# Split weight slots moved from 64 to 48 bytes above the split activations in the address modulo 256, in a two-block transformer kernel

## The chip, the cores and the metric

One core of a Trainium2 chip runs the whole program. The time is the device time of one execution in microseconds. Where a number is called a profiled one it comes from a single execution taken by the hardware profiler.

## What is computed

The reference runs two small models one after the other on one sequence of 256 tokens and 1024 features, all in float32. Nearly all the arithmetic is in products of a 256-row activation with a weight matrix of 1024 or 2816 rows:

```python
def first_block(x, ...):              # layer 0: fox attention, layer 1: NSA attention
    h = rmsnorm(x, norm_g[i])
    y = fox_mixer(...) or nsa_mixer(...)   # h @ w_in, attention, o @ w_out
    x = x + y
...
def _conv_ffn(h, w_up, conv_w, conv_b, w_down):   # after an HGRN mixer and after an MLA mixer
    u = h @ w_up                       # 1024 -> 2 x 2816
    y = causal 3-tap convolution of u
    gate, up = jnp.split(y, 2, axis=-1)
    return (jax.nn.silu(gate) * up) @ w_down       # 2816 -> 1024
```

## The kernel before, in words

**Tiling.** Features lie on the 128 partitions, so `x`, `h` and the split copies `h_high` and `h_low` are tensors of 128 partitions by 8 chunks by 256 tokens. Weights are streamed as 138 tiles of 1 MB or somewhat less (128 partitions by 2048 columns of float32). The tile numbered t uses slot t modulo 3 (`NSLOT`) of three tensors: `ring` (what the DMA writes), `w_high` and `w_low`.

**The split.** To keep float32 accuracy with the one-pass float32r format, each operand a is cut into a high part (rounded to float32r) and a low part (a minus the high part). For the weights, ScalarE writes the high part (`high`, line 399), VectorE the low part (`low`, line 409, or in halves, line 418). For activations this is done once per norm or per output. `product3` (lines 444 to 449) then issues three TensorE matmuls into one PSUM accumulator: high by high (L447), high by low (L448), low by high (L449). Each has its own load of a 128 by 128 stationary operand, which TensorE does beside the matmul before it, and a moving operand of 256 columns.

**Which operand stands and which moves.** `by_feature` and the two FFN routines hold the weights stationary and move the activations; in the trace these are the tile pairs `h_high,w_high`, `ffn_hidden_high,w_high` and the like (moving operand first). `by_token` holds the activations stationary and moves the weights (`w_high,h_high`).

**What sets the order.** The order is written out by hand for every engine. SP issues the load of tile t when the low part of tile t-3 has been made (`load`, line 363 and before; `load_ffn` in the FFN loop). ScalarE makes the high part of tile t when the load has landed and TensorE has finished tile t-3 (`tile_done`). VectorE makes the low part after it. TensorE waits for the low part (`in_parts`) and for a free PSUM bank. Stages follow one another: fox, NSA, HGRN, FFN 0, MLA, FFN 1.

**Where the tensors lie.** The allocator places tensors in the order of the calls of `sb` in `build` (from line 151 on) and starts each at the next multiple of 32 bytes in the partition. By adding up the sizes, the start addresses are (bytes in the partition, and modulo 256): `h_high` 32896 (128), `h_low` 41088 (128), `eps` 49280, `scratch` 49312, `w_high` 49344 (192), `w_low` 73920 (192), `ring` 98496 (192), `cst` 123072 (192), and the working area with all other split activations (`fox_out`, `blocks`, `hgrn_out`, `ffn_hidden`, `mla_out`, `lora`, `levels`) at addresses that are 128 modulo 256. Chunks and slots step by whole multiples of 256 bytes, so each tensor keeps its remainder throughout. The split weights therefore stand 64 bytes above every split activation modulo 256.

Of the kernel before, what the change touches and what calls it, by code (L numbers as in the profile page):

```python
# [17 lines left out]
F32R = mybir.dt.float32r  # L18
# [6 lines left out]
P = 128  # L25
# [25 lines left out]
NSLOT = 3  # L51
SLOT = 2048
# [88 lines left out]
def build(nc, A, cst_dram, out, at):  # L141
    ctx = ExitStack()
    with ctx:
        def sb(name, shape, dt=F32):
            return ctx.enter_context(nc.sbuf_tensor(name, shape, dt))
# [6 lines left out]
        h = sb("h", [P, DC, S])  # L152

        h_hi, h_lo = sb("h_high", [P, DC, S], F32R), sb("h_low", [P, DC, S], F32R)
        eps, scratch = sb("eps", [P, 1]), sb("scratch", [P, 1])
        w_hi, w_lo = sb("w_high", [P, NSLOT, SLOT], F32R), sb("w_low", [P, NSLOT, SLOT], F32R)
        ring = sb("ring", [P, NSLOT, SLOT])
        ncst = at["levels"][0]
        cst = sb("cst", [P, ncst])
# [2803 lines left out]
```

How the kernel before makes its waits and increments, by code:

```python
    def __call__(self, ins):  # L135
        self.n += 1
        ins.then_inc(self.sem, 1)
        self.eng.wait_ge(self.sem, self.n)
# [217 lines left out]
        def load(sp, t):  # L356
            if t >= NT:
                return
            if t >= NSLOT:
                sp.wait_ge(low_in[t % NSLOT], t // NSLOT)
            src = tiles[t]
            s = w_loaded[t % NSLOT]
            if src[0] == "up":
# [17 lines left out]
        def landed(eng, t, later=0):  # L382
            eng.wait_ge(w_loaded[t % NSLOT], later * 32 + 16 * (t // NSLOT + 1))
# [3 lines left out]
        def high(act, t, later=0, ops=None):  # L388
            if t >= NT:
                return
            landed(act, t, later)
            if tiles[t][0] == "q_up":
                act.wait_ge(q_swapped[tiles[t][2]], 80)
            if t >= NSLOT:
                act.wait_ge(tile_done, later * 6 + t - NSLOT + 1)
            dst, src = w_hi[:, t % NSLOT, :], ring[:, t % NSLOT, :]
            if ops is None:
                i = nc.scalar.activation(dst, src, ACT.Copy)
            else:
                i = ops.tensor_copy(dst, src)
            i.then_inc(high_in[t % NSLOT], 1)
# [1 line left out]
        def low(eng, ops, t, later=0):  # L404
            if t >= NT:
                return
            eng.wait_ge(high_in[t % NSLOT], later * 2 + t // NSLOT + 1)
            ops.tensor_tensor(w_lo[:, t % NSLOT, :], ring[:, t % NSLOT, :], w_hi[:, t % NSLOT, :].bitcast(F32),
                              ALU.subtract).then_inc(low_in[t % NSLOT], 1)
```

## Time and profile before

| | us |
|---|---|
| median of 3 runs | 1025.72 |
| lowest and highest run | 1021.55 and 1028.17 |
| profiled execution, its own time | 1021.83 |
| profiled span, first to last instruction | 1020.0 |
| TensorE matmul busy in the span | 986.8 |
| weight load busy | 938.1 |
| VectorE, ScalarE, GpSimd busy | 767.8, 549.8, 65.8 |

The page's busy time of TensorE counts overlapping matmuls once: each matmul record is some 0.28 us long, but the next begins some 0.115 us after it began. The distance between starts, not the length of a record, is what one more matmul costs in a stream, and it is read from the timeline or from the number of matmuls in a window. The clock column gives the share of 2.4 GHz that was granted.

### The profile page before, as it was taken

To read this page: it belongs to the slowest core of one execution; us is meant where nothing else is said; L and a number is where in the kernel's file an instruction comes from. 1 tells how busy PE (TensorE), PEld (TensorE's weight loads), DVE (VectorE), ACT (ScalarE), POOL (GpSimd) and SP (SyncE) were. 2 spreads that over 40 slices of the span, in tenths; PEclk is the share of its full clock that TensorE was granted. 3 is DMA by queue.
4 is the path that set the end of the run, shared out by engine and by line. 5 is a ranking of instruction groups with operands and counts; after the bars stand their busy time and mean duration, and the time that the engine had idled before them with its cause. 6 is when DMAs were issued, how large, how long until landed. Compare 5 with 4: busy or idle time off the path is not lost. (4 is left out here: it accounts for less than half of the span.)

```text
span 1020.0 us, 20361 instructions
## 1 busy us (share of the span) xinstructions
PE 986.8 (97%) x8176; PEld 938.1 (92%) x8178; DVE 767.8 (75%) x1300; ACT 549.8 (54%) x869; POOL 65.8 (6%) x54
## 2 busy tenths in 40 slices
PE   7999999999999999999999999999999999999997
PEld 5999999897778999899999999999998899999996
DVE  5766776867787678598657978788876759888885
ACT  5545555364766656543555545454765556545541
POOL 4000004000000400000030000000000430000000
PEclk9999999999999999999999999999999999999999
DMA  8544435893112557400455766665531347765741
GB/s 281 173 130 147 137 126 150 246 287 99 63 43 84 165 172 215 152 1 16 151 166 145 216 176 195 175 201 170 151 124 42 85 124 206 207 206 170 217 149 42
DMA packets 184141, 153.08 MB, mean 150 GB/s; under 512 B 12477, under 2 KB 176900, under 8 KB 184068
## 3 DMA queue, kind: packets, MB, share of 16 engines
q1 hardware_dynamic: 183858, 152.01, 49.9%
q8 instruction: 51, 0.84, 0.3%
q14 instruction: 22, 0.18, 0.1%
q10 hardware_dynamic: 210, 0.05, 0.0%
HBM read 148.91 MB, written 1.05 MB: 147 GB/s over the span
## 5 line engine op out<-in xcount | busy, mean ns | idle before, releaser
L447 PE MATMUL bank<-h_high,w_high 128*128 128x256 f32 x1312 | 373.2, 284 | 8.3 <-DVE ffn_normed L1096 3.4
L448 PE MATMUL bank<-h_low,w_high 128*128 128x256 f32 x1312 | 365.7, 279 | 0.0
L449 PE MATMUL bank<-h_high,w_low 128*128 128x256 f32 x1312 | 365.6, 279 | 0.0
L399 ACT ACTIVATE w_high<-ring 128x2048 fp32r<-128x2048 f32 x137 | 261.7, 1913 | 136.8 <-PE bank L449 130.4
L409 DVE TENSOR_TENSOR w_low<-ring,w_high 128x2048 fp32r<-128x2048 f32 x118 | 271.4, 2301 | 26.9 <-ACT w_high L399 26.6
L447 PEld LDWEIGHTS bank<-h_high,w_high 128*128 128x128 f32 x1312 | 247.4, 189 | 11.2 <-issue 6.4
L448 PEld LDWEIGHTS bank<-h_low,w_high 128*128 128x128 f32 x1312 | 248.9, 190 | 0.5 <-issue 0.5
L449 PEld LDWEIGHTS bank<-h_high,w_low 128*128 128x128 f32 x1312 | 247.4, 189 | 0.0
L447 PE MATMUL bank<-ffn_hidden_high,w_high 128*128 (+1 forms) x352 | 98.2, 279 | 2.8 <-DVE ffn_hidden_low L1129 2.8
L448 PE MATMUL bank<-ffn_hidden_low,w_high 128*128 (+1 forms) x352 | 98.0, 279 | 0.0
L449 PE MATMUL bank<-ffn_hidden_high,w_low 128*128 (+1 forms) x352 | 98.0, 279 | 0.0
L1083 ACT ACTIVATE ffn_conv<-ffn_normed,par 128x256 f32<-128x256 f32 x88 | 48.1, 594 | 73.9 <-DVE ffn_normed L1096 73.9
L1105 DVE SCALAR_TENSOR_TENSOR ffn_conv<-ffn_normed,par,ffn_conv 128x254 f32<-128x254 f32 (+1 forms) x176 | 77.0, 480 | 7.4 <-ACT ffn_conv L1083 2.3
L796 ACT ACTIVATE work<-bank,work 128x128 f32<-128x128 f32 (+1 forms) x112 | 47.7, 432 | 48.2 <-DVE work L778 36.7
L447 PEld LDWEIGHTS bank<-ffn_hidden_high,w_high 128*128 128x128 f32 x352 | 66.1, 188 | 3.2 <-issue 3.2
L611 POOL TENSOR_TENSOR h<-h 128x512 f32<-128x512 f32 x15 | 38.4, 2558 | 461.2 <-ACT h L594 460.9
L448 PEld LDWEIGHTS bank<-ffn_hidden_low,w_high 128*128 128x128 f32 x352 | 66.8, 190 | 0.0
L449 PEld LDWEIGHTS bank<-ffn_hidden_high,w_low 128*128 128x128 f32 x352 | 66.1, 188 | 0.0
L758 PE MATMUL bank<-work 128*128 128x256 f32 (+2 forms) x160 | 54.3, 440 | 2.7 <-ACT work L796 2.6
L418 DVE TENSOR_TENSOR w_low<-ring,w_high 128x1024 fp32r<-128x1024 f32 x40 | 48.5, 1220 | 5.8 <-ACT w_high L399 5.8
L778 DVE TENSOR_REDUCE work<-bank 128x2 f32<-128x256 f32 (+2 forms) x64 | 32.3, 504 | 22.5 <-PE bank L763 22.0
L447 PE MATMUL bank<-w_high,h_high 128*128 128x256 f32 x160 | 46.0, 287 | 2.9 <-DVE w_low L409 2.9
(352 smaller groups left out, 1735.1 us busy)
## 6 DMA issues: line engine op xcount, KB each, us to landing
ring<-in_ffn_w_up_dram SPq DMA_DIRECT2D x44, 1024.0 KB, 6.0
ring<-in_ffn_w_down_dram SPq DMA_DIRECT2D x22, 1024.0 KB, 5.0
ring<-in_fox_w_in_dram SPq DMA_DIRECT2D x16, 1024.0 KB, 5.9
ring<-in_hgrn_w_in_dram SPq DMA_DIRECT2D x16, 1024.0 KB, 5.6
ring<-in_nsa_w_in_dram SPq DMA_DIRECT2D x14, 1024.0 KB, 5.5
ring<-in_fox_w_out_dram SPq DMA_DIRECT2D x4, 1024.0 KB, 5.0
ring<-in_nsa_w_out_dram SPq DMA_DIRECT2D x4, 1024.0 KB, 5.0
ring<-in_hgrn_w_out_dram SPq DMA_DIRECT2D x4, 1024.0 KB, 5.0
```

The lines of the kernel that those rows point to most:

```text
L399: i = nc.scalar.activation(dst, src, ACT.Copy)
L409: ops.tensor_tensor(w_lo[:, t % NSLOT, :], ring[:, t % NSLOT, :], w_hi[:, t % NSLOT, :].bitcast(F32), ALU.subtract).then_inc(low_in[t % NS ...
L418: i = nc.vector.tensor_tensor(w_lo[:, t % NSLOT, q], ring[:, t % NSLOT, q], w_hi[:, t % NSLOT, q].bitcast(F32), ALU.subtract)
L447: nc.tensor.matmul(o, ah, bh, start=start, stop=False, **kw)
L448: nc.tensor.matmul(o, ah, bl, start=False, stop=False, **kw)
L449: return nc.tensor.matmul(o, al, bh, start=False, stop=stop, **kw)
L611: ops.tensor_tensor(h[:, 0:2, :], h[:, 0:2, :], h[:, 2 * i:2 * i + 2, :], ALU.add).then_inc(n_added, 1)
L758: nc.tensor.matmul(o, q, k, start=(i == 0), stop=False)
L778: i = nc.vector.tensor_reduce(least, self.bank(u), AX.X, ALU.min)
L796: i = nc.scalar.activation(pb[:, e, 0:unit["w"]], ps[:, e, :], ACT.Exp, scale=unit["scale"][1] if unit.get("scale") else -1.0, bias=self.l ...
L1083: i = nc.scalar.activation(y[:, j % 2, e, :], un[:, j % 2, e, :], ACT.Identity, scale=column(cw + 4 * FC, e, j, later), bias=column(cb, e, ...
L1105: i = nc.vector.scalar_tensor_tensor(out=dst, in0=un[:, j % 2, e, 0:S - back], scalar=column(cw + (2 - back) * 2 * FC, e, j, later), in1=d ...
```

## The change

One buffer `w_parts` takes the place of `w_high` and `w_low`. It is allocated directly after `h_low`, ahead of `eps` and `scratch`, and holds 12 unused columns (48 bytes), then the three high slots, then the three low slots.

```diff
         h_hi, h_lo = sb("h_high", [P, DC, S], F32R), sb("h_low", [P, DC, S], F32R)
+        w_both = sb("w_parts", [P, 12 + 2 * NSLOT * SLOT], F32R)
+        w_hi, w_lo = [w_both[:, 12 + i * NSLOT * SLOT:12 + (i + 1) * NSLOT * SLOT].rearrange("p (k n) -> p k n", k=NSLOT)
+                      for i in range(2)]
         eps, scratch = sb("eps", [P, 1]), sb("scratch", [P, 1])
-        w_hi, w_lo = sb("w_high", [P, NSLOT, SLOT], F32R), sb("w_low", [P, NSLOT, SLOT], F32R)
         ring = sb("ring", [P, NSLOT, SLOT])
```

No instruction, wait or semaphore is added or removed. Addresses move as follows. The high slots start at 49280 + 48 = 49328 and the low ones at 73904, both 176 modulo 256. `w_parts` ends at 98480, `eps` goes to 98496, `scratch` to 98528 and `ring` to 98560 (0 modulo 256), so that `ring` and every tensor allocated after it lies 64 bytes higher than before. The working area, with all split activations but `h_high` and `h_low`, is then at 192 modulo 256. The split weights stand 48 bytes above `h_high` and `h_low` and 16 bytes below the other split activations, modulo 256.

## Rows read from the trace of the kernel before

**Rows 1.** The page, its head: busy time, share of span, instructions.
```profile
span 1020.0 us, 20361 instructions
PE 986.8 (97%) x8176; PEld 938.1 (92%) x8178; DVE 767.8 (75%) x1300; ACT 549.8 (54%) x869; POOL 65.8 (6%) x54
```
**Rows 2.** Waits of TensorE by line, the largest: total us, times, longest us.
```profile
PE bank L447 <- DVE w_low L409: 4.5, 2, 2.9
```
**Rows 3.** Windows: length, PE (x), PEld, DVE, ACT, POOL, clock, DMA.
```profile
600.00:650.00 50.00, 50.00 (x427) 50.00 (x426) 39.97 (x57) 25.50 (x27) 0.00 (x0) 1.00 0.64 184
...
850.00:900.00 50.00, 50.00 (x443) 50.00 (x442) 44.91 (x64) 27.34 (x30) 0.00 (x0) 1.00 0.69 204
```
**Rows 4.** Timeline of TensorE in FFN 0: start us, length us, instruction.
```profile
600.11 0.28 PE L447 MATMUL bank<-h_high,w_high 128*128 128x256 f32 x1
...
601.17 0.28 PE L447 MATMUL bank<-h_high,w_high 128*128 128x256 f32 x1
```
**Rows 5.** The same in FFN 1.
```profile
899.90 0.28 PE L447 MATMUL bank<-h_high,w_high 128*128 128x256 f32 x1
...
900.92 0.28 PE L447 MATMUL bank<-h_high,w_high 128*128 128x256 f32 x1
```
**Rows 6.** Timeline of TensorE, activations stationary, in NSA.
```profile
181.79 0.28 PE L447 MATMUL bank<-w_high,h_high 128*128 128x256 f32 x1
...
182.81 0.28 PE L447 MATMUL bank<-w_high,h_high 128*128 128x256 f32 x1
```
**Rows 7.** The same in HGRN.
```profile
404.75 0.28 PE L447 MATMUL bank<-w_high,h_high 128*128 128x256 f32 x1
...
405.81 0.28 PE L447 MATMUL bank<-w_high,h_high 128*128 128x256 f32 x1
```
**Rows 8.** Windows counting L449 alone, one per product: length, PE (x), clock, DMA.
```profile
0.00:1020.00 1020.00, 604.62 (x2168) 1.00 0.50 150
16.29:21.71 5.42, 4.18 (x15) 1.00 0.71 224
...
401.00:423.36 22.36, 17.64 (x64) 1.00 0.65 197
549.35:713.06 163.71, 130.10 (x464) 1.00 0.65 189
...
847.65:1004.84 157.19, 127.56 (x463) 1.00 0.60 176
1006.94:1012.36 5.42, 4.21 (x15) 1.00 0.00 0
```
**Rows 9.** Groups by line, shapes apart: count, busy us, mean ns, idle before; products on h.
```profile
L447 PE MATMUL bank<-h_high,w_high 128*128 128x256 f32 x1312 | 373.2, 284 | 8.3 <-DVE ffn_normed L1096 3.4 <-DVE w_low L409 1.6 <-DVE work L1944 1.5
...
L447 PE MATMUL bank<-w_high,h_high 128*128 128x256 f32 x160 | 46.0, 287 | 2.9 <-DVE w_low L409 2.9
```
**Rows 10.** Timeline: one-column matmuls, each with a full 128-column weight load.
```profile
354.20 0.58 PE L627 MATMUL bank<-cst,h 128*128 128x1 f32 x4
...
355.53 0.58 PE L627 MATMUL bank<-cst,work 128*128 128x1 f32 x4
```
**Rows 11.** Timeline: 512-column float32r matmuls, both operands 128 modulo 256.
```profile
427.79 0.40 PE L2172 MATMUL bank<-levels,hgrn_out_low 128*128 128x512 f32 x1
...
428.25 0.39 PE L2172 MATMUL bank<-levels,hgrn_out_low 128*128 128x512 f32 x1
```
**Rows 12.** Groups by line: writers of the slots, and two other VectorE groups.
```profile
L409 DVE TENSOR_TENSOR w_low<-ring,w_high 128x2048 fp32r<-128x2048 f32 x118 | 271.4, 2301 | 26.9 <-ACT w_high L399 26.6
...
L399 ACT ACTIVATE w_high<-ring 128x2048 fp32r<-128x2048 f32 x137 | 261.7, 1913 | 136.8 <-PE bank L449 130.4 <-DMA ring<-in_nsa_w_in_dram 4.8 <-DMA ring<-in_hgrn_w_in_dram 0.8
...
L1105 DVE SCALAR_TENSOR_TENSOR ffn_conv<-ffn_normed,par,ffn_conv 128x255 f32<-128x255 f32 x88 | 38.5, 479 | 2.3 <-ACT ffn_conv L1083 2.3
...
L586 DVE SCALAR_TENSOR_TENSOR h_low<-x,par,h_high 128x256 fp32r<-128x256 f32 x40 | 17.3, 482 | 15.3 <-ACT h_high L580 15.3
```
**Rows 13.** DMA issues of the page: ring tiles, KB each, median us to landing.
```profile
ring<-in_ffn_w_up_dram SPq DMA_DIRECT2D x44, 1024.0 KB, 6.0
```

## The prediction

> **What bounds the kernel now.** I read the head of the page first. TensorE has a matmul in flight for 986.8 of 1020.0 us, and VectorE, the next busiest, for 767.8 [rows 1]. The list of waits says the same from the other side: the largest group of TensorE's waits is 4.5 us in two waits [rows 2]. In the windows, stretches of 50 us in both FFN stages are covered by matmuls from end to end at a granted clock of 1.00, that is 2.4 GHz [rows 3]. So TensorE's stream sets the end, and what can move the time is the distance from one matmul start to the next.
>
> That distance is what the reader should look at. In FFN 0 nine matmuls begin between 600.11 and 601.17 us, 1.06 / 9 = 117.8 ns each [rows 4]. In FFN 1 the same nine lie between 899.90 and 900.92, 1.02 / 9 = 113.3 ns [rows 5]. Shape, line, granted clock and, by the allocation, addresses are the same in both. The windows confirm it for whole stages: 464 products of three matmuls in 163.71 us are 117.6 ns each, 463 products in 157.19 us are 113.2 ns (a count takes in the ones cut at the edges) [rows 8]. Where the activations are the stationary operand both values occur too: 1.02 / 9 = 113.3 in one place [rows 6], 1.06 / 9 = 117.8 in another [rows 7]. I call them the fast and the slow rhythm. A stream keeps its rhythm until it is interrupted: there is nothing in between.
>
> Neither is what 256 columns cost, 256 / 2.4 = 106.7 ns. The fast rhythm lies 6.7 ns above it, the slow one 11.1 ns.
>
> How much of each is there? Taking the sum of three successive distances all through the timeline, of the 3 x 2168 = 6504 matmuls of L447 to L449 [rows 8], 3252 stand in the fast rhythm, 2711 in the slow one, and 541 at an interruption or a change of shape. The first slow stretch begins at 16.29 us, the last at 1006.94; the two longest stretches are FFN 0, slow, and FFN 1, fast, and of the middle ones the 64 products from 401.00 us are slow [rows 8].
>
> **The change, part by part.** Instructions, waits and queues stay as they are; only addresses differ. Four effects follow.
>
> First, the pace of the products on `h`. They are 1312 + 160 of 2168 products, 68% [rows 8, 9]. During each of their matmuls TensorE reads 256 columns of one operand and loads 128 of the other, from places that were 64 bytes apart modulo 256 and will be 48 apart. Both reads go on at once, one at twice the rate in columns of the other, so they pass through equal remainders twice in each matmul. If the excess over 106.7 ns comes from such meetings, their timing depends on this distance. The trace of before has no row at 48, so I bound it from both sides. Below: matmuls of one column, each with a full load and almost no second reader, follow one another at (355.53 - 354.20) / 12 = 110.8 ns [rows 10]; no stream with a load for each matmul should be faster. Above: float32r matmuls of 512 columns with both operands at the same remainder take (428.25 - 427.79) / 2 = 230 ns [rows 11] where 512 / 2.4 = 213.3, so the excess for one load is 16.7 ns, and at a difference of 0 a 256-column matmul would take 106.7 + 16.7 = 123.4. The excess is thus 16.7 ns at a difference of 0 and 6.7 or 11.1 ns at 64: that is the one sign in this trace that the distance matters. 48 is nearer to 64 than to 0. I take the fast rhythm, 113.3 ns: of the values between the two ends it is the one that the same instructions already show for hundreds of products, and a start in steps of less than 64 bytes is the simplest way in which the slow one could cease.
>
> Second, the pace of the other 696 products, whose distance goes from 64 above to 16 below. The same bounds hold: 110.8 and 123.4 ns. 16 is near 0, which speaks for the upper end; I still take 113.3, with less confidence, since the 512-column rows have another ratio of columns to load.
>
> Sum of the two: 2711 slow matmuls x (117.8 - 113.3 = 4.44 ns, from 0.04 us in 9) = 12.0 us less. The 541 at interruptions are left as they are.
>
> The Trainium skill (TensorE: Matmul & The Clock Gate, section Back-to-back issue gap) gives 256 / 2.4 + 2.5 = 109.2 ns for an isolated warm stream. Neither rhythm reaches it here. By it all 5963 matmuls in a rhythm would have 4 to 8.6 ns to give, 37 us in all; the sum above doesn't use it.
>
> Third, the writers of the slots. They now start 16 bytes past a multiple of 32. VectorE at a start that is one column (4 bytes) off takes 479 ns for 255 columns, against 482 ns for 256 columns at an aligned start [rows 12]. I take 0 for its low parts. For ScalarE's high part no row shows an odd start; its bound below is 0, and above I use its cover. An FFN tile is 48 matmuls, 48 x 113.3 = 5.44 us, and three slots give 16.3 us for a round. One round is the matmuls of the tile, 5.44, then the high part, 1.91, then the low part, 2.30 [rows 12], together 9.65 us: 6.7 us are spare. VectorE is busy for 44.91 of 50 us in the fast FFN [rows 3]; at 110.8 ns it would be 92% busy, still not the bound. Without this cover a tenth more on each low part would cost 138 x 0.23 = 32 us.
>
> Fourth, `ring` and everything behind it lie 64 bytes higher, the ring at 0 instead of 192. A 1 MB tile lands in 6.0 us [rows 13]; landing, high and low part are 6.0 + 1.9 + 2.3 = 10.2 us of the 16.3 us that pass until the slot's next tile is due. Landings could double before TensorE felt it. 0 us. The attention stages keep their differences within the working area; only those between it and `cst`, both moved by 64, and `x` or `h` change. Few matmuls read both, 0 us.
>
> The profiled execution took 1021.83 us, 3.9 us less than the median of 1025.72. 1021.83 - 12.0 = 1009.8, about 1010 us. If the excess of the median is more slow rhythm, as the size suggests (one FFN stage of 1392 matmuls turning from slow to fast is 6.2 us, and the runs spread over 6.6), it goes as well, so I don't scale to the median.
>
> **Rivals.**
>
> *The rhythm does not know the distance (no change).* For it speaks that both rhythms occur at one and the same distance [rows 4, 5] and in both roles [rows 6, 7]: something at the start of a stream picks them, not the address. Against it speaks the larger excess at a difference of 0. Then the share of slow matmuls is drawn anew, and the time stays between 1018 and 1029 us, most likely 1024. The Trainium skill (SBUF — State Buffer, section Who interferes with whom) is on this side: TensorE has two independent read ports, one for the moving operand and one for the weight load, and never waits on anyone. The trace fits that only in part, since 113.3 and 117.8 ns are both above the 110.8 ns of loads alone.
>
> *The other rhythm becomes the only one (slower).* The distance matters, but 48 or -16 favours the slow rhythm. 3252 x 4.44 = 14.4 us more, 1036 us. This decides as soon as more than 2711 + 400 matmuls are slow. For it: the slow rhythm is nearly the only one where activations are stationary, where the distance has the other sign, in the long stretch from 401 us for instance [rows 7, 8].
>
> *Split.* `h` gains and the others lose: 68% of 12.0 is 8.2 us less; the other 696 x 3 = 2088 matmuls, now at 115.3 on average, go to 117.8, 5.2 us more, or to 123.4, 16.9 us more. 1019 to 1031 us, in the middle 1025.
>
> *All excess goes.* 110.8 ns everywhere: 2711 x 7.0 + 3252 x 2.5 = 27.1 us less, 995 us; on `h` alone 18.4 us less, 1003.
>
> **How the numbers follow.** Fast rhythm throughout, 1010 us (own range 1005 to 1015): 0.34. No change: 0.28. Slow rhythm: 0.16. Split: 0.12. All excess goes: 0.10. The range from 998 to 1036 leaves out half of the last case, half of the slow one and a little of the split, some 0.15. A difference of 1% is about what a measurement of this kernel can tell from none, since its runs spread over 0.65%; from 1025.72 the bounds are 1015.5 and 1036.0. Faster: the first and the last case, 0.44. Slower: half of the slow case and the worst of the split, about 0.12. Within 1%: 0.44.
>
> **What the profile after would show.** If the first step is right, every stretch of `h_high` against the high slots has 9 matmuls in 1.02 us, in FFN 0 too, and the window of FFN 0 is some 6 us shorter. If the second is right, so do `ffn_hidden`, `blocks` and `mla_out`; if the split is right, the two tile pairs differ within FFN 0. If the distance doesn't matter, both rhythms are there with both tile pairs. ScalarE's L399 at 1913 ns and VectorE's L409 at 2301 ns should stay within 1%; a mean that rises shows the third step wrong. The prediction fails if a third rhythm appears, or if the choice of rhythm is a matter of chance.

## The result and the profile after

| | before | after |
|---|---|---|
| median, us | 1023.63 (4 runs) | 1036.08 (4 runs) |
| lowest and highest, us | 1015.39 and 1028.17 | 1033.64 and 1037.78 |
| profiled execution, us | 1021.83 | 1037.78 |

The ratio is 1.0124 (95% interval 1.0081 to 1.0167): the change makes the kernel 1.2% slower. The forecast was 1010 us, 1.2% below the profiled execution of before.

The head of the page of the kernel after, to be held against [rows 1]:

```profile
span 1036.0 us, 20363 instructions
PE 1007.7 (97%) x8178; PEld 958.6 (93%) x8178; DVE 766.7 (74%) x1300; ACT 549.6 (53%) x869; POOL 68.6 (7%) x54
```

TensorE's busy time grew by 20.9 us. ScalarE and VectorE are within 1.1 us of before; GpSimd's grew by 2.8 us, with 68.6 of 1036.0 us still far from any limit. Next the windows of the kernel after (columns as in [rows 3]), and its waits of TensorE (as in [rows 2]):

```profile
600.00:650.00 50.00, 50.00 (x426) 50.00 (x425) 40.78 (x57) 24.55 (x26) 0.00 (x0) 1.00 0.58 183
900.00:950.00 50.00, 50.00 (x425) 50.00 (x424) 40.01 (x55) 25.52 (x27) 0.00 (x0) 1.00 0.59 184
```
```profile
PE bank L449 <- DVE w_parts L411: 3.5, 2, 2.9
PE bank L449 <- DVE ffn_normed L1098: 2.8, 4, 0.8
```

TensorE is still covered from end to end at a granted clock of 1.00 (2.4 GHz), and none of its larger waits has grown. But the fast FFN 1 of before, 443 matmuls in 50 us [rows 3], is gone: both stages now have about 425. To see the pace of the products alone, I count the first line of `product3`, one per product, in the main part of FFN 0 and FFN 1. The columns are window, length, busy (count), clock, DMA share and GB/s. The kernel before:

```profile
570.00:705.00 135.00, 107.35 (x383) 1.00 0.65 191
872.00:1002.00 130.00, 105.53 (x383) 1.00 0.61 178
```

and the kernel after:

```profile
570.00:705.00 135.00, 106.98 (x382) 1.00 0.61 189
872.00:1002.00 130.00, 102.88 (x367) 1.00 0.62 194
```

With three matmuls per product: FFN 0 goes from 117.5 to 117.8 ns per matmul, FFN 1 from 113.1 to 118.1. The timeline shows what the matmuls do one by one. Columns are start, length and instruction; the lines are nine matmuls apart. The kernel after, on `h` in HGRN, on `h` in FFN 0, and on the FFN's hidden activations in FFN 1:

```profile
404.83 0.28 PE L450 MATMUL bank<-h_low,w_parts 128*128 128x256 f32 x1
...
405.94 0.29 PE L450 MATMUL bank<-h_low,w_parts 128*128 128x256 f32 x1
...
610.01 0.28 PE L450 MATMUL bank<-h_low,w_parts 128*128 128x256 f32 x1
...
611.08 0.28 PE L450 MATMUL bank<-h_low,w_parts 128*128 128x256 f32 x1
...
949.86 0.28 PE L450 MATMUL bank<-ffn_hidden_low,w_parts 128*128 x1
...
950.91 0.28 PE L450 MATMUL bank<-ffn_hidden_low,w_parts 128*128 x1
```

1.11 / 9 = 123.3 ns, 1.07 / 9 = 118.9 ns and 1.05 / 9 = 116.7 ns. Before had two values, 113.3 and 117.8 [rows 4 to 7]. After has many more between 116.7 and 125.7 (per product, that is from one L449 to the next: 350, 353.5, 356, 363 and 377 ns among others), and 113.3 ns, 340 per product, does not occur once. The single distances changed too: in the slow rhythm of before nearly all are 117 to 119 ns, after they range from 113 to 130, and in HGRN 117 and 130 take turns. (The timeline prints hundredths of a microsecond; these were read from the nanoseconds in the trace.)

The balance for the whole span: I add up, product by product, the time from its first matmul to the first of the next, wherever two products follow each other directly. Products without an interruption (under 380 ns) are 1959 before and take 677.8 us; they are 1960 after and take 696.4 us, 18.6 us more. All the others, those at interruptions, take 72.8 us before and 69.7 after. The sum is 15.5 us more, and the span grew by 16.0. So the loss is in the pace of the undisturbed stream, 115.3 ns per matmul before and 118.4 after.

### The profile page after: what moved, and what is told of

It reads as the page before. It is cut to its first block and busy times, and to the rows that moved or that the text cites. A ratio compares the mean times of both kernels' runs of the same rounds, so it can differ in the third digit from the quotient of the medians.

```text
span 1036.0 us, 20363 instructions
## 1 busy us (share of the span) xinstructions
PE 1007.7 (97%) x8178; PEld 958.6 (93%) x8178; DVE 766.7 (74%) x1300; ACT 549.6 (53%) x869; POOL 68.6 (7%) x54
## 3 DMA queue, kind: packets, MB, share of 16 engines
HBM read 148.91 MB, written 1.05 MB: 145 GB/s over the span
## 5 line engine op out<-in xcount | busy, mean ns | idle before, releaser
L449 PE MATMUL bank<-h_high,w_parts 128*128 128x256 f32 x1312 | 376.9, 287 | 6.3 <-DVE ffn_normed L1098 2.8
L450 PE MATMUL bank<-h_low,w_parts 128*128 128x256 f32 x1312 | 369.5, 282 | 0.0
L451 PE MATMUL bank<-h_high,w_parts 128*128 128x256 f32 x1312 | 369.4, 282 | 0.0
L401 ACT ACTIVATE w_parts<-ring 128x2048 fp32r<-128x2048 f32 x137 | 261.6, 1912 | 151.2 <-PE bank L451 147.1
L411 DVE TENSOR_TENSOR w_parts<-ring,w_parts 128x2048 fp32r<-128x2048 f32 x118 | 271.0, 2298 | 30.1 <-ACT w_parts L401 29.6
L449 PEld LDWEIGHTS bank<-h_high,w_parts 128*128 128x128 f32 x1312 | 248.9, 190 | 8.8 <-issue 5.9
L450 PEld LDWEIGHTS bank<-h_low,w_parts 128*128 128x128 f32 x1312 | 249.2, 190 | 0.5 <-issue 0.5
L451 PEld LDWEIGHTS bank<-h_high,w_parts 128*128 128x128 f32 x1312 | 248.8, 190 | 0.0
L449 PE MATMUL bank<-ffn_hidden_high,w_parts 128*128 (+1 forms) x352 | 98.7, 280 | 2.2 <-DVE ffn_hidden_low L1131 2.2
L450 PE MATMUL bank<-ffn_hidden_low,w_parts 128*128 (+1 forms) x352 | 98.5, 280 | 0.0
L451 PE MATMUL bank<-ffn_hidden_high,w_parts 128*128 (+1 forms) x352 | 98.5, 280 | 0.0
L449 PEld LDWEIGHTS bank<-ffn_hidden_high,w_parts 128*128 128x128 f32 x352 | 66.1, 188 | 2.6 <-issue 2.6
L450 PEld LDWEIGHTS bank<-ffn_hidden_low,w_parts 128*128 128x128 f32 x352 | 66.1, 188 | 0.0
L451 PEld LDWEIGHTS bank<-ffn_hidden_high,w_parts 128*128 128x128 f32 x352 | 66.0, 188 | 0.0
L449 PE MATMUL bank<-w_parts,h_high 128*128 128x256 f32 x160 | 47.0, 294 | 2.9 <-DVE w_parts L411 2.9
L780 DVE TENSOR_REDUCE work<-bank 128x2 f32<-128x256 f32 (+2 forms) x64 | 32.2, 504 | 23.4 <-PE bank L765 22.8
```

The source lines that it names most:

```text
L401: i = nc.scalar.activation(dst, src, ACT.Copy)
L411: ops.tensor_tensor(w_lo[:, t % NSLOT, :], ring[:, t % NSLOT, :], w_hi[:, t % NSLOT, :].bitcast(F32), ALU.subtract).then_inc(low_in[t % NS ...
L449: nc.tensor.matmul(o, ah, bh, start=start, stop=False, **kw)
L450: nc.tensor.matmul(o, ah, bl, start=False, stop=False, **kw)
L451: return nc.tensor.matmul(o, al, bh, start=False, stop=stop, **kw)
L780: i = nc.vector.tensor_reduce(least, self.bank(u), AX.X, ALU.min)
```

## The experiments

After the result four theories stood. **D, distance**: the pace follows from the distance between the two operands modulo 256. **S, start**: a start that is not a multiple of 64 bytes costs, whatever the distance. **B, both places**: it takes both places, modulo 256, to fix the pace. **C, chance**: the rhythm is drawn at the start of each stream, whatever the addresses. Beside them the ring and working area, which the change moves by 64 bytes, could have a part in it (**R** in the expectations). Some later expectations also speak of **M**: the two reads of TensorE, for the load and for the moving operand, get in each other's way.

### Streams of products alone

Three small kernels, with the model's computation left out: streams of 48 matmuls of the same form as in `product3`, six streams for each of sixteen distances, in random order and with a random pause between them. A pace below is that of a stream's last 41 intervals. The core of all of them (a cut from the kernel, which differs from the model's kernel almost everywhere):

```diff
+DISTANCES = [0, 16, 32, 48, 64, 80, 96, 112, 128, 144, 160, 176, 192, 208, 224, 240]
+a = [w[:, h * 1024 + c * P:h * 1024 + (c + 1) * P] for h in range(2)]   # stationary
+b = [v[:, c, :] for v in (a_hi, a_lo)]                                  # moving, 256 columns
+product3(B[s % 4][:, j * S:(j + 1) * S], a, b, c == 0, c == DC - 1)
```

**Weights stationary, activations at 128.**

> A kernel that leaves the whole computation out and only runs streams of 48 product matmuls (weights stationary, activations moving at 128 modulo 256) from weight buffers that stand 0, 16, ..., 240 bytes above the activations modulo 256, 6 streams each in mixed order, each begun after a short wait of random length. Theory D (the distance of the two reads modulo 256 sets which rhythms exist): at 64 both 113.3 and 117.8 ns appear, at 48 none below 117.5, at 240 (that is -16) a mix of 116.5 to 121. Theory S (a weight slot that starts off a multiple of 64 bytes is slow, whatever the distance): 113.3 appears at 0, 64, 128 and 192 alike and at none of the other twelve. Theory C (chance: addresses don't matter): all sixteen distances show the same mix.

**Weights moving, activations stationary at 128.** (`a` and `b` change roles.)

> The same with the roles exchanged: activations stationary, weights moving, so that the stationary operand stands below the moving one by the distance; the computation is left out. Theory D: the table of the sweep before, read with the sign of the distance changed (192 here behaves as 64 there). Theory S: 113.3 ns at 0, 64, 128 and 192 only. Theory C: the same mix everywhere.

**As the first, both operands 16 bytes further** (`ACT_AT = 144` for 128).

> The first sweep again with activations and weights both 16 bytes further on (activations at 144 modulo 256), so that the distances are the same and no operand starts on a multiple of 64 bytes; the computation is left out. Theory D: the same table as the first sweep, 113.3 ns at a distance of 64 included. Theory S: at a distance of 64 nothing below 117 ns; 113.3 moves to the distances 48, 112, 176 and 240, where the weight buffer starts on a multiple of 64. If both starts matter, 113.3 is nowhere.

Measured, the mean of six streams in ns per matmul:

| distance | stationary, 128 | moving, 128 | stationary, 144 |
|---|---|---|---|
| 0 | 120.0 | 120.0 | 118.4 |
| 16 | 118.3 | 116.8 | 117.1 |
| 32 | 118.4 | 116.9 | 120.0 |
| 48 | 118.0 | 118.3 | 118.8 |
| 64 | 114.8 | 117.8 | 113.6 |
| 112 | 120.0 | 113.8 | 118.0 |
| 144 | 118.9 | 118.4 | 113.6 |
| 160 | 120.0 | 118.2 | 120.0 |
| 192 | 117.8 | 114.1 | 116.7 |
| 240 | 118.2 | 117.1 | 117.3 |

(The other six distances lie between 116.7 and 120.0.) At distance 64 and activations at 128, the layout of before, four of the six streams ran at 113.34 ns and two at 117.78: both rhythms of [rows 4, 5], from the same code, with VectorE and the DMA queues idle beside it. The timeline of the first of these kernels, one line each nine matmuls: a stream at 64, another at 64, one at 48, one at 0.

```profile
68.05 0.28 PE L61 MATMUL bank<-act,w_above 128*128 128x256 f32 x1
...
69.07 0.28 PE L61 MATMUL bank<-act,w_above 128*128 128x256 f32 x1
...
252.73 0.28 PE L61 MATMUL bank<-act,w_above 128*128 128x256 f32 x1
...
253.79 0.28 PE L61 MATMUL bank<-act,w_above 128*128 128x256 f32 x1
...
29.27 0.28 PE L61 MATMUL bank<-act,w_above 128*128 128x256 f32 x1
...
30.33 0.28 PE L61 MATMUL bank<-act,w_above 128*128 128x256 f32 x1
...
86.95 0.28 PE L61 MATMUL bank<-act,w_above 128*128 128x256 f32 x1
...
88.03 0.28 PE L61 MATMUL bank<-act,w_above 128*128 128x256 f32 x1
```

1.02 / 9 = 113.3, 1.06 / 9 = 117.8, 1.06 / 9 = 117.8 and 1.08 / 9 = 120.0 ns. Theory S falls: with activations at 144 and weights at 208 (a distance of 64) all six streams are fast, 113.3 to 113.8 ns. D falls: distance 144 costs 118.9 with activations at 128 and 113.6 with activations at 144. The two roles don't agree either, not even with the sign of the distance changed: distance 144 with the weights stationary has 118.9, and 112 with the weights moving has 113.8. C falls as a whole, but a part of it stays: the addresses decide which rhythms are open to a stream, and at some of them (64 at 128) the start still picks between two. B stands, together with this remainder of chance. At distance 48 no stream was at 113.3 in any of the three kernels; the fastest of the 18 had 116.6.

**48 bytes above all split activations, nothing else moved.** `eps` and `scratch` go into the small row-norm tensors, so that the ring and the working area lie as before; all splits stay at 128, the slots at 176.

```diff
-        eps, scratch = sb("eps", [P, 1]), sb("scratch", [P, 1])
-        rstd, rstd_half, rstd_in = [sb(n, [P, TT]) for n in ("rstd", "rstd_half", "rstd_inner")]
+        wide = [sb(n, [P, 8]) for n in ("rstd", "rstd_half", "rstd_inner")]
+        rstd, rstd_half, rstd_in = [v[:, 0:TT] for v in wide]
+        eps, scratch = [v[:, TT:TT + 1] for v in wide[:2]]
```

> The whole kernel with the slots at 176 modulo 256 as in the changed one, and with ring, constants and the working area left where they were (all split activations at 128): 48 above every one of them. Theory D: no matmul of a product at 113.3, all at the rhythms that the changed kernel has for h_high (353.7, 355.6 and 363 ns for three), 118.1 ns on average, time 1035 us. Theory S: also slower, 1034 to 1037, since the slots start off a multiple of 64. Theory R (what cost the time is the move of ring and working area by 64 bytes): 1022 to 1026 us, as before.

Measured: 1042.17 us against 1021.59, ratio 1.0196 (1.0122 to 1.027). So the move of the ring and of the working area is not the cause (R expected 1022 to 1026 us): with both undone the loss is larger, not smaller. It is also 7 us larger than the 1035 us that D expected. Its undisturbed products take 698.9 us, 2.5 more than after, and as after none of them is at 340 ns. Its windows, counted as above, have 383 products in FFN 0, as many as before in its slow rhythm, and 367 in FFN 1:

```profile
570.00:705.00 135.00, 106.40 (x383) 1.00 0.66 192
872.00:1002.00 130.00, 103.36 (x367) 1.00 0.66 191
```

With the weights stationary, the products on `blocks` and `fox_out` have a mean of 123.3 and 122.3 ns, where 16 below gave 117.3 for both; `hgrn_out` alone is better at 48 (117.8 against 119.5). No stream by itself was that slow at 48, so the kernel has something here that the streams lack; I did not find out what. One difference is that the streams run with the other engines and the DMA queues almost idle, while in the kernel these read and write the same memory at the same time. No run tells whether this matters.

### Maps of both places

**Every place of the activations with every place of the weights**, in steps of 16 bytes, two streams of 24 matmuls each, the computation left out again. All pairs use one weight buffer and one activation buffer. A pace below is that of a stream's last 20 intervals; with fewer of them a cell moves by some tenths of a nanosecond, at distances 64 and 144 by up to 1.2. Weights stationary:

```diff
+GRID = list(range(0, 256, 16))
+STREAMS = 2
+pairs = [(a, w) for a in GRID for w in GRID]
```

> The computation is left out: streams of 24 product matmuls, weights stationary, for every one of 16 places of the activations (0, 16, ..., 240 modulo 256) with every one of 16 places of the weights, two streams each in mixed order. Theory D (distance alone): the 16 pairs of one distance agree with each other, 64 the fastest. Theory B (both places count, the distance being only one view of them): pairs of one distance differ by several ns, and 113.3 to 113.8 ns stands in a few cells, among them (144, 208) and (144, 32) as in the sweep at 144.

Weights moving:

> The same map with activations stationary and weights moving; the computation is left out. Theory D: one value for each distance. Theory B: it differs along a distance; (128, 240) is near 113.8 as in the sweep before, (128, 192) near 117.8.

Measured: no cell of either map is below 113.3 ns, and the slowest of each is at 120.2 and 120.8. With the weights stationary, distance 64 is at 113.3 to 115.7 in all sixteen places and has the best mean, 114.3; at some places 192 or 144 matches or beats it (activations at 32, 80 or 208: 113.3 at distance 192). 160 is at 119.7 to 120.0 in all places, 48 at 117.8 to 119.1, and 144 is either 114.5 to 115.4 or 118.2 to 120.0 by place. With the weights moving, 192 has the best mean (113.5 to 117.7 by place) and 96 is always at 119.8 to 120.0. So the distance does much and the place the rest, and the layout of before was already on the best diagonal of the first map. With two streams for a cell, a cell shows a rhythm that is open there, but not that no other is.

**Distance 0**, by taking the 12 columns away (slots and all splits at 128):

```diff
-        w_both = sb("w_parts", [P, 12 + 2 * NSLOT * SLOT], F32R)
+        w_both = sb("w_parts", [P, 0 + 2 * NSLOT * SLOT], F32R)
```

(The 12 in the two slices that follow becomes 0 as well, and 16 in the next.)

> The whole kernel with no column in front: slots at 128 modulo 256, at distance 0 from every split activation; ring, constants and working area as before. From the sweep at 128 (120.0 ns in all six streams) theories D and B: 5963 matmuls x (120.0 - 115.3) = 28 us more, 1049 us. Theory S (only a start off a multiple of 64 is slow): as before, 1018 to 1027.

**16 columns in place of 12**: the slots are back at 64 above `h`, and everything behind them, the other splits too, lies 64 bytes higher, so that their distance to the slots is 0.

```diff
-        w_both = sb("w_parts", [P, 12 + 2 * NSLOT * SLOT], F32R)
+        w_both = sb("w_parts", [P, 16 + 2 * NSLOT * SLOT], F32R)
```

> The changed kernel with 16 columns in front in place of 12: slots at 192 modulo 256 as before the change, 64 above h; ring, constants and working area 64 bytes higher, so that the other split activations are at distance 0. Theories D and B: h_high at 113.3 and 117.8 again, ffn_hidden, blocks and the others near 120: 2088 x 4 ns = 8 us more, 1030. Theory S: as before, 1018 to 1027. Theory R (move of the ring): 1034 to 1038 as with 12 columns.

Measured: distance 0 takes 1045.99 us against 1021.97, ratio 1.0237 (1.0182 to 1.0293), 3 us below the 1049 that both D and B gave, and far from the 1018 to 1027 of S. 16 columns take 1024.8, ratio 1.003 (1.0004 to 1.0055). In the kernel with distance 0 the rhythm is 360 ns per product almost everywhere (1852 of 1962 undisturbed products): a single value, and no fast one to draw. Its windows, counted as above:

```profile
570.00:705.00 135.00, 106.12 (x376) 1.00 0.65 188
872.00:1002.00 130.00, 102.16 (x361) 1.00 0.65 189
```

With 16 columns the two pairs part within one kernel: with the weights stationary, products on `h` are at 114.6 ns and those on the other splits, now at distance 0, at 119.3 to 120.0. The expectation of 1030 was some 5 us too high, though hardly in the products: undisturbed, they take 6.9 us more than before, where 8 was expected. `h` gave back 2.1 us of it (805 of its 1168 undisturbed products with the weights stationary stand at 340 ns, 649 of 1162 before); most of the rest of the miss, 3.4 us, lies in the products at interruptions.

### A layout from the map

There are places where distance 64 showed no slow rhythm in any stream: with activations at 144 it was 113.3 to 113.8 ns in the six streams of the sweep and 113.9 and 114.1 in the two of the map. **Splits at 144, slots at 208**: a helper allocates each pair of halves in one buffer with columns in front (a cut; the other splits go the same way).

```diff
+        def two_parts(t, off, n, pattern, **dims):
+            return [t[:, off + i * n:off + (i + 1) * n].rearrange(pattern, **dims) for i in range(2)]
+        h_both = sb("h_parts", [P, 4 + 2 * DC * S], F32R)
+        h_hi, h_lo = two_parts(h_both, 4, DC * S, "p (c n) -> p c n", c=DC)
+        w_hi, w_lo = two_parts(w_both, 12, NSLOT * SLOT, "p (k n) -> p k n", k=NSLOT)
...
+                self.at = 4          # all other splits: 4 columns in front of each pair
```

> The whole kernel with every split activation at 144 modulo 256 and the slots at 208, 64 above all of them, no operand on a multiple of 64 bytes; the working area begins 16 bytes later, eps and scratch lie in one tensor with the row norms. From the map and the sweep at 144 (113.3 to 113.9 ns in all eight streams) theory B expects the 117.8 ns rhythm to be gone where weights are stationary: 113.65 ns instead of 115.2, and about 116 where activations are; together 5963 x 1.6 = 9.5 us less than before, 1012 us, and a smaller spread of the runs. Theory S expects it slower than before, since no slot starts on a multiple of 64. Theory D expects both rhythms as before, 1018 to 1027.

**Splits at 144, slots at 184** (6 columns in front of the slots), a distance of 40 that the sweep in 4-byte steps below had shown to be fast. By adding up the sizes, the ring and the constants lie 32 bytes higher than before in the first of the two kernels and where they were in the second.

> As with slots at 208, but with the slots at 184, 40 bytes above every split activation. The sweep in steps of 4 bytes had 113.34 ns in all six streams there, against 113.3 to 113.7 at 208, so where weights are stationary 113.35 ns; where activations are, no row yet, 116 to 120. Theory B: 1010 to 1014 us, 0.6 to 0.8% below the kernel before, spread of the runs under 4 us. Theory D and S: both put it where the change was (48 above, off a multiple of 64), 1034 to 1042.

Measured: 1014.62 us against 1017.98, ratio 0.9949 (0.992 to 0.9977), and 1015.03 against 1020.83, ratio 0.995 (0.9923 to 0.9976). Both are faster than the kernel before, by half a per cent. The runs of the first spread over 3.7 us (12 runs) where those of before spread over 13.6 (17 runs). The spread alone is no proof of a single rhythm, though: with 16 columns, where `h` has both, ten runs spread over 3.0 us. The windows of the first in the same view, FFN 0 only since FFN 1 ends earlier here, and its head:

```profile
570.00:705.00 135.00, 109.20 (x398) 1.00 0.68 198
```
```profile
span 1012.0 us, 20363 instructions
PE 979.0 (97%) x8178; PEld 929.6 (92%) x8178; DVE 767.1 (76%) x1300; ACT 550.5 (54%) x869; POOL 65.9 (7%) x54
```

398 products against 383: 135 / 1194 = 113.1 ns. 1656 of its 1957 undisturbed products stand at 340 to 342 ns. The expectations were met in direction but not in size: 1014.62 us where 1012 was expected, and with 184 1015.03 where 1010 to 1014 was, with a spread of 4.8 us in place of under 4. Part of it is that where the weights move, the pace stayed at 118.4 ns and did not fall to 116; in the kernel with 184 it is 119.9. A layout has to serve both roles, and this one serves the weights stationary alone.

### What of the distance and of the load counts

Five more small kernels, the computation left out in each. **Loads of 64 columns** in the first one's streams (each stationary operand cut to its first half; the matmul then also writes 64 rows of the bank in place of 128, so load and output shrink together):

```diff
-a = [w[:, h * 1024 + c * P:h * 1024 + (c + 1) * P] for h in range(2)]
+a = [w[:, h * 1024 + c * P:h * 1024 + c * P + 64] for h in range(2)]
```

> The first sweep again (activations at 128, sixteen distances, six streams each), but every weight load has 64 columns in place of 128 and the matmul writes 64 rows; the computation is left out. If the excess over 106.7 ns is the two reads getting in each other's way (theory M), half the load's reads leave about half the excess and half the differences: 109 to 114 ns. If the pace is set by the load alone, matmuls being bound by it, the pace falls to what 256 columns need by themselves, one value near 109 ns at all distances.

**Steps of 4 bytes** around 64, activations at 144 (`DISTANCES = [36, 40, ... 92]`):

> The computation is left out: activations at 144 modulo 256, weights stationary at distances from 36 to 92 in steps of 4 bytes, six streams each. 64 should be at 113.6 again. If what counts are blocks of 16 bytes, the four distances that begin in one block agree (52 to 60 as at 48, 64 to 76 as at 64). If a start within a block costs an extra read, 64 stands alone at 113.6 and its neighbours are above 116. If the place counts to the byte, a distance better than 113.3 may lie between.

**Loads of 8 columns** (`c * P + 8`, with 8 rows written):

> The sweep at 128 with loads of 8 columns in place of 128, the computation left out: next to nothing is read for the load while the matmul streams. Theory M (the two reads get in each other's way): the differences between distances go, the pace is one value near 109 ns or at most 113.3. If it is the moving read by itself that pauses, and the place of the activations is what counts, one value again, but above 113. If differences of several ns between distances stay, the meeting of long reads is not the cause.

**bf16 operands** at the same places (`F32R` to `BF16` for both):

> The sweep at 128 with bf16 operands at the same byte places, the computation left out: half the bytes for the same columns. Theory M: with half the bytes of both reads the pace is one value near 109 ns at all sixteen distances, for it is the 4-byte moving operand at 2.4 GHz that crowds the memory. If the rhythms are something of TensorE's own pipeline, 113.3 and 117.8 ns appear here too.

**Steps of 4 bytes with the weights moving**, activations at 144:

> The computation is left out: activations stationary at 144, weights moving at distances from 36 to 92 in steps of 4 bytes. At 64 about 116 (115.9 in the map), at 40 unknown. Theory B: neighbours 4 bytes apart differ by up to 6 ns, and some distance has 113.3 to 113.9. Theory D: the values of the stationary sweep at the distance with the other sign.

Measured:

*Half loads.* Neither expectation. The floor stays at 113.3 ns (distance 0, all streams), the rest lies between 113.8 and 119.1, and the order of the distances is another: 0, the worst with full loads, is now the best, and 64 is at 117.2. Halving the load does not halve the excess; it changes which distances are fast.

*Steps of 4 bytes.* 36: 118.4, 40: 113.3 (all six streams), 44: 118.6, 48: 119.2, 52: 118.9, 56: 119.6, 60: 119.6 (four streams at 117.8, two at 123.3), 64: 113.5, 68: 120.0. One column more or less makes 5 to 7 ns, so blocks of 16 bytes are not what counts. No distance was below 113.3. The timeline of a stream at 40 and of one at 48:

```profile
134.76 0.28 PE L61 MATMUL bank<-act,w_above 128*128 128x256 f32 x1
...
135.78 0.28 PE L61 MATMUL bank<-act,w_above 128*128 128x256 f32 x1
...
147.31 0.29 PE L61 MATMUL bank<-act,w_above 128*128 128x256 f32 x1
...
148.38 0.28 PE L61 MATMUL bank<-act,w_above 128*128 128x256 f32 x1
```

1.02 / 9 = 113.3 and 1.07 / 9 = 118.9 ns.

*Loads of 8 columns.* Most streams are at 113.3, but 116.7 and 120.0 still occur, at most distances and now by stream: at 192 the streams had 113.3, 113.6, 116.7 and 120.0. Two streams at distance 64:

```profile
193.88 0.28 PE L61 MATMUL bank<-act,w_above 128*8 128x256 f32 x1
...
194.90 0.28 PE L61 MATMUL bank<-act,w_above 128*8 128x256 f32 x1
...
445.01 0.28 PE L61 MATMUL bank<-act,w_above 128*8 128x256 f32 x1
...
446.06 0.28 PE L61 MATMUL bank<-act,w_above 128*8 128x256 f32 x1
```

1.02 / 9 = 113.3 and 1.05 / 9 = 116.7 ns. By the test set in the expectation this speaks against M as it was put: with next to no load, means by distance still differ by 3.6 ns (113.35 at 112, 116.98 at 16, where no stream had 113.3). What the runs do show is that the length of the load changes which distances are slow and how firmly: with 128 columns 160 is at 120.0 in all six streams, with 8 three of its six are at 113.3. A set of rhythms, 113.3, 116.7 and 120.0, is there with almost no load.

*bf16.* The sixteen means are 109.17 to 109.19 ns, and every one of the 96 streams is between 109.15 and 109.20. Its timeline at distance 48:

```profile
94.09 0.27 PE L61 MATMUL bank<-act,w_above 128*128 128x256 bf16 x1
...
95.07 0.27 PE L61 MATMUL bank<-act,w_above 128*128 128x256 bf16 x1
```

0.98 / 9 = 108.9 ns, to the rounding of the view. No rhythms and no addresses in this sweep (weights stationary, activations at 128): what was seen above belongs to float32r there. Whether it is its 4 bytes or its format that counts is open, since bf16 changes both. The Trainium skill (TensorE: Matmul & The Clock Gate, section Back-to-back issue gap) has N / 2.4 + 2.5 ns for the isolated gap of one warm matmul, 109.2 ns for 256 columns. These bf16 streams, each matmul with a load of its own, agree to 0.1 ns; float32r never reaches it. The prediction called this the figure of an isolated stream, which is more than the page says.

*Weights moving, steps of 4 bytes.* Distance 40 is at 120.0, 64 at 115.8 (three streams at 113.3, three at 118.3), the rest between 116.7 and 121.7. Neighbours differ by up to 5.8 ns as expected; the other half of the expectation, a distance with 113.3 to 113.9, was missed, since even 64 has 113.3 in only half of its streams. This is where the kernel with slots at 184 has its 119.9 ns from.

## Why the prediction was wrong, step by step

**What bounds the kernel: right.** The start-to-start distance of the product matmuls carried the whole difference, in every full kernel. The undisturbed products, in us for the whole span, beside the span itself, each as a difference to before:

| | slots above `h` / above the others | products | span |
|---|---|---|---|
| after | 48 / -16 | +18.6 | +16.0 |
| only the distance, 48 | 48 / 48 | +21.1 | +20.0 |
| 12 columns away | 0 / 0 | +28.0 | +22.8 |
| 16 columns | 64 / 0 | +6.9 | +2.2 |
| splits 144, slots 208 | 64 / 64 | -8.3 | -8.0 |

The two columns differ by up to 5.2 us, mostly because the products at interruptions took less time (4.8 us less with 12 columns away); I did not follow up why. TensorE's mean granted clock was 0.994 after and 0.996 before: its granted clock fell to the lower level, 1.2 GHz, for 3.4 us three times after and twice before (the last 1.5 us of both spans aside). One such stretch more is at most 1.7 us of the 16.0.

**First step, the pace on `h`: failed.** This is the step that decided the forecast. It took 48 to be like 64, "48 is nearer to 64 than to 0", and put the fast rhythm there, 113.3 ns. It rested on the idea that the pace changes smoothly with the distance between two ends known from before. It doesn't. At 4-byte steps 40 and 64 are fast and 44 to 60 are slow; in the kernel after `h` runs at 118.5 ns with the weights stationary (115.2 before), where 113.3 was taken. Over the 1168 undisturbed products of this kind, 3504 matmuls, 3.3 ns each are 11.6 of the 18.6 us. The upper bound of 123.4 ns, from the 512-column rows [rows 11], was too high for distance 0, which measures 120.0, but not high enough for all places: 55 products of the kernel after stand at 376 or 377 ns, 125.6 per matmul. The lower bound of 110.8 [rows 10] was never approached by float32r: none of the 512 cells of the maps is below 113.3. Nor is it what it was called, a pace that no stream with a load for each matmul beats, since bf16 ran at 109.2 with such loads; its rows are of plain float32 operands (`h` and a constant), a third type.

**Second step, the other splits: failed the same way.** At 16 below they run at 117.3 to 119.5 ns, by tensor. The doubt put down there ("speaks for the upper end") pointed the right way; the measured values lie about midway between 113.3 and the upper end, 123.4.

**Third and fourth step: right.** The groups of the writers in the kernel after, against [rows 12], and its DMA issues, against [rows 13]:

```profile
L401 ACT ACTIVATE w_parts<-ring 128x2048 fp32r<-128x2048 f32 x137 | 261.6, 1912 | 151.2 <-PE bank L451 147.1
L411 DVE TENSOR_TENSOR w_parts<-ring,w_parts 128x2048 fp32r<-128x2048 f32 x118 | 271.0, 2298 | 30.1 <-ACT w_parts L401 29.6
...
ring<-in_ffn_w_up_dram SPq DMA_DIRECT2D x44, 1024.0 KB, 5.6
```

1912 for 1913 ns, 2298 for 2301, 5.6 for 6.0 us. ScalarE's idle time ahead of its high part grew from 136.8 to 151.2 us, nearly all of it spent waiting for TensorE to finish a slot (147.1 us): it follows the pace of TensorE and costs nothing itself.

**The rivals.** The price of the slow rhythm, 1036 us, was met to 0.1 us, but not by its mechanism, and that is luck: of the 1960 undisturbed products of the kernel after only 390 have all three distances at the 117 to 119 ns of the slow rhythm. The others follow new patterns, and the mean of all is 118.4 ns, which happens to be near 117.8. The prediction's own sign of failure, that a third rhythm appears, is what came about. Its *Split*, with `h` gaining and the others losing, did not: `h` lost as well. It took the kernel with 16 columns to part the two. The rival "the rhythm does not know the distance" is refuted by the maps. Its evidence was real, since at 64 the start does pick one of two; but this says that at this place two rhythms are open, not that the place doesn't matter. The Trainium skill (SBUF — State Buffer, section Who interferes with whom) has TensorE's two read ports, for the moving operand and for the load, independent, and has TensorE never wait on anyone. For bf16 the sixteen distances fit that; for float32r the same streams range from 113.3 to 120 ns by address alone, and here the measurement decides. That the two reads wait for each other is not shown by this; only the pace was seen.

**The size of the gain that was sought: right, apart from one role.** 4.44 ns for each slow matmul is what the layout at 144 and 208 collects: its undisturbed products take 8.3 us less than those of the profiled execution of before. Of the 12.0 us of the sum the missing part is mostly where the weights move: 118.4 ns there in place of 113.3, some 2.6 us. In the medians the gain is smaller, 3.4 us (5.8 with the slots at 184). A likely reason is that before draws its share of slow stretches anew in each run, so that the profiled one need not be typical; those runs left no trace, so this is not shown.

**What stays open.** Why a pair of places has just these rhythms, what at the start of a stream picks one where two are open, and why the full kernels have rhythms (377 ns per product) that are slower than any stream alone (at most 123.3 ns per matmul against 125.6). That 113.3 ns is the floor for float32r is what 512 pairs of places showed at 16-byte steps; at 4-byte steps only fifteen distances at one place of the activations were looked at. That addresses count modulo 256, and not by some other period, was taken for granted and never tested. The cause inside TensorE or the memory was not seen by any view, only its dependence on addresses, on the length of the load and on the operands' type.

## What to carry to other kernels

Where one engine is covered from end to end, look at the distances between its starts before its waits: two rhythms of the same instruction are a reserve, and a spread of the runs without a wait to explain it can be a sign of them. But a layout can't be reasoned from two known points: the pace jumps between neighbouring 4-byte places, so measure the streams alone, over both operands' places and in both roles, and then the kernel, before keeping a move. Here half a per cent was there to gain and 2.4% to lose.

## What the runs showed of the hardware that was not expected

The load of the stationary operand has a record of its own, and its length depends on the type. The groups with shapes apart (columns as in [rows 9]) of the small kernels: float32r with 128 columns,

```profile
L62 PEld LDWEIGHTS bank<-act,w_above 128*128 128x128 f32 x1536 | 289.3, 188 | 0.0
```

with 64 columns,

```profile
L62 PEld LDWEIGHTS bank<-act,w_above 128*64 128x64 f32 x1536 | 206.4, 134 | 0.1
```

with 8 columns,

```profile
L62 PEld LDWEIGHTS bank<-act,w_above 128*8 128x8 f32 x1536 | 135.0, 88 | 39.2
```

and bf16 with 128:

```profile
L62 PEld LDWEIGHTS bank<-act,w_above 128*128 128x128 bf16 x1536 | 150.1, 98 | 16.8
```

From 8 to 64 columns a float32r load grows by 46 ns, 0.82 ns per column, and from 64 to 128 by 54, 0.84 per column: about two cycles of 2.4 GHz for each column. By that slope 128 columns are some 107 ns (an estimate), as long as the 256 moving columns beside them at one per cycle (106.7). The whole record of the bf16 load is 98 ns, 90 less. It would fit both that a float32r matmul has a load and a stream that each fill nearly its whole time, so that a delay of either goes into the pace, and that bf16 has no rhythms. But this is an argument and no measurement: it was not tested apart from the type, the loads of 64 and of 8 columns leave the floor of 113.3 ns where it was, and with 8 columns some of the slower rhythms stay.
